# A two-layer hybrid decoder in float32: where the matmuls' moving operands stand in SBUF

## The reference, cut to what matters

```python
for layer in range(2):
    h = rmsnorm(x, g[0])
    m = mixer_ab(h, ...) if layer == 0 else mixer_cd(h, ...)
    x = x + rmsnorm(m, g[1])
    h = rmsnorm(x, g[2])
    x = x + rmsnorm(cross_attn(h, mem, wq, wkv, wo), g[3])   # 4 heads of 256
    h = rmsnorm(x, g[4])
    r = relu(h @ w1)                                         # 1024 -> 4096
    x = x + rmsnorm((r * r) @ w2, g[5])                      # 4096 -> 1024
```

## The kernel before

| moving operand, against | before | after |
|---|---|---|
| `h` (normed x; attention output), `w` | 448 | 448 |
| `r` (squared ReLU), `w` | 384 | 448 |
| `mem` (memory tokens), `w` (keys) | 256 | 448 |
| `mh`, `ml` (mixer C and D outputs), `w` | 256 | 448 |
| `my` (gated), `mp` (pooled), `w` | 320 | 448 |
| `k`, against `q` | 128 | 448 |
| `pt`, against `v` | 448 | 448 |
| `w`, against `mem` (values) | 256 | 64 |

## Time and profile before

### The profile page before, as it was taken

One profiled execution on the slowest core, in us unless ns is written; L12 is line 12 of the kernel. 1 busy time (PEld: TensorE's weight loads), 2 busy tenths in 40 slices (PEclk: granted clock), 3 DMA queues, 4 the chain that ended last, 5 costly groups with the idle time before them and its releaser, 6 DMA issues.

```text
span 960.5 us, 17149 instructions
## 1 busy us (share of the span) xinstructions
PE 902.9 (94%) x7268; PEld 878.1 (91%) x7268; DVE 667.1 (69%) x1030; ACT 472.7 (49%) x661; POOL 268.6 (28%) x195
## 2 busy tenths in 40 slices
PE   6999998899989999999999988999998699999997
PEld 6899988798979999999799988899898699999996
DVE  6897988777287555555779999967676385555553
ACT  5545544565355444444553333646464364454543
POOL 1000817243142000000468687346341340000000
PEclk9999999999999999999999999999999899999999
DMA  8454434544455555655555554245442445655551
GB/s 286 133 176 133 149 114 134 174 133 132 132 175 182 192 189 186 195 186 183 162 165 181 180 173 125 96 137 169 156 133 88 132 132 182 202 191 193 190 184 45
DMA packets 81031, 153.74 MB, mean 160 GB/s; under 512 B 6251, under 2 KB 7227, under 8 KB 80955
## 3 DMA queue, kind: packets, MB, share of 16 engines
q1 hardware_dynamic: 80843, 152.60, 49.9%
q10 hardware_dynamic: 112, 0.05, 0.0%
HBM read 151.58 MB, written 1.05 MB: 159 GB/s over the span
## 4 chain that ended last, share of the span: by engine, by line
PE 64%; DVE 24%; ACT 4%; issue 3%; POOL 3%; DMA 2%; DVEq 0%; POOLq 0%; ACTq 0%
PE ps L501 20%; PE ps L503 20%; PE ps L502 19%; DVE ps L1643 5%; DVE w_lo L1279 4%; ACT w_hi L927 2%; POOL w_lo L1916 2%; DVE E L1450 1%; DVE xc L1351 1%; DMA raw<-in_mlp_w 1%; DVE xT L1591 1%; PE ps L743 1%; PE ps L745 1%; PE ps L744 1%; PE ps L568 1%
## 5 line engine op out<-in xcount | busy, mean ns | idle before, releaser
L927 ACT ACTIVATE w_hi<-raw 128x1024 fp32r<-128x1024 f32 x284 | 296.9, 1055 | 255.8 <-DMA raw<-in_mlp_w 138.4
L501 PE MATMUL ps<-h_hi,w_hi 128*128 128x256 f32 x1280 | 363.8, 284 | 27.9 <-issue 13.7
L1279 DVE TENSOR_TENSOR w_lo<-raw,w_hi 128x1024 fp32r<-128x1024 f32 x210 | 274.1, 1324 | 129.5 <-ACT w_hi L927 129.3
L502 PE MATMUL ps<-h_lo,w_hi 128*128 128x256 f32 x1280 | 360.9, 282 | 0.0
L503 PE MATMUL ps<-h_hi,w_lo 128*128 128x256 f32 x1280 | 360.9, 282 | 0.0
L501 PEld LDWEIGHTS ps<-h_hi,w_hi 128*128 128x128 f32 x1280 | 247.1, 193 | 31.9 <-issue 17.8
L502 PEld LDWEIGHTS ps<-h_lo,w_hi 128*128 128x128 f32 x1280 | 247.3, 193 | 0.0
L503 PEld LDWEIGHTS ps<-h_hi,w_lo 128*128 128x128 f32 x1280 | 247.1, 193 | 0.0
L1916 POOL TENSOR_TENSOR w_lo<-raw,w_hi 128x1024 fp32r<-128x1024 f32 x74 | 183.0, 2494 | 99.4 <-ACT w_hi L927 99.4
L1939 POOL TENSOR_TENSOR rfac<-stat,mhalf 128x2 f32<-128x2 f32 (+1 forms) x14 | 16.6, 1182 | 457.1 <-DVE stat L1573 326.1
L501 PE MATMUL ps<-r_hi,w_hi 128*128 128x256 f32 x512 | 144.3, 282 | 0.0
(11 more groups left out here) (247 smaller groups left out, 1291.7 us busy)
## 6 DMA issues: line engine op xcount, KB each, us to landing
raw<-in_mlp_w SPq DMA_DIRECT2D x128, 512.0 KB, 3.8
raw<-in_cd_w_in SPq DMA_DIRECT2D x40, 512.0 KB, 3.7
raw<-in_xa_wkv SPq DMA_DIRECT2D x32, 512.0 KB, 4.0
raw<-in_ab_w_in SPq DMA_DIRECT2D x24, 512.0 KB, 3.9
raw<-in_xa_wq SPq DMA_DIRECT2D x16, 512.0 KB, 3.8
raw<-in_xa_wo SPq DMA_DIRECT2D x16, 512.0 KB, 3.8
raw<-in_cd_w_out SPq DMA_DIRECT2D x16, 512.0 KB, 3.7
raw<-in_ab_w_out SPq DMA_DIRECT2D x12, 512.0 KB, 3.8
```

The costliest lines, as they stand in the source:

```text
L501: nc.tensor.matmul(dst, wt[0], x[0], start=start, stop=False, skip_group_check=True)
L502: nc.tensor.matmul(dst, wt[0], x[1], start=False, stop=False, skip_group_check=True)
L927: nc.scalar.activation(w_hi[:, v % SLOTS, :, :], raw[:, v % SLOTS, :, :], ACT.Copy)\
L1279: V.tensor_tensor(w_lo[:, v % SLOTS, :, :], raw[:, v % SLOTS, :, :], f(w_hi[:, v % SLOTS, :, :]), ALU.subtract).then_inc(lo_ready_dve, 1)
```

## The change

It moves tensors and does nothing else: `mhalf` (8 floats) goes ahead of the memory tokens, and the unused bytes are placed anew, so that the places are those of the table's last column. No instruction is added, removed or moved in order.

```diff
--- before.py
+++ after.py
@@ -291,9 +291,9 @@
             raw = sb("raw", [SLOTS, 2, 512], scope=s)
         w_lo = sb("w_lo", [SLOTS, 2, 512], F32R)
         xT = sb("xT", [J, T])
-        skip(256)
+        mhalf = sb("mhalf", [8])
+        skip(416)
         mem_hi, mem_lo = sb("mem_hi", [J, T], F32R), sb("mem_lo", [J, T], F32R)
-        skip(192)
         h_hi, h_lo = sb("h_hi", [J, T], F32R), sb("h_lo", [J, T], F32R)
         k_hi, k_lo = sb("k_hi", [J, T], F32R), sb("k_lo", [J, T], F32R)
 
@@ -304,9 +304,7 @@
         Ssum, S2 = sb("Ssum", [H2]), sb("S2", [T])
         stat = sb("stat", [16, 8])
         rfac = sb("rfac", [16, 8])
-        mhalf = sb("mhalf", [8])
         tmp = sb("tmp", [2, T])
-        skip(352)
 
         with ExitStack() as s:
             v_hi, v_lo = sb("v_hi", [TT, D], F32R, s), sb("v_lo", [TT, D], F32R, s)
@@ -342,18 +340,19 @@
         with ExitStack() as s:
             vpad = sb("vpad", [J, T + 30], scope=s)
             cv, cv3 = sb("cv", [J, T], scope=s), sb("cv3", [J, T], scope=s)
+            skip(64, s)
             mh, ml = sb("mh", [2 * J, T], F32R, s), sb("ml", [2 * J, T], F32R, s)
             ppad = sb("ppad", [2, 2, T + 2], scope=s)
             sg = sb("sg", [4, T], scope=s)
             Rsq = sb("Rsq", [T], scope=s)
             sct = sb("sct", [2, H2], scope=s)
         with ExitStack() as s:
+            skip(64, s)
             q_hi, q_lo = sb("q_hi", [J, T], F32R, s), sb("q_lo", [J, T], F32R, s)
             prob = sb("prob", [4, TT, T], scope=s)
-            skip(448, s)
+            skip(384, s)
             pt_hi, pt_lo = sb("pt_hi", [4, TT, T], F32R, s), sb("pt_lo", [4, TT, T], F32R, s)
         with ExitStack() as s:
-            skip(64, s)
             r_hi, r_lo = sb("r_hi", [2, 4, T], F32R, s), sb("r_lo", [2, 4, T], F32R, s)
             relu, rsq = sb("relu", [2, H2], scope=s), sb("rsq", [2, H2], scope=s)
             otok = sb("otok", [TT, D], scope=s)
```

## The result

| | before | changed |
|---|---|---|
| median of 18 runs | 960.62 us | 964.87 us |
| lowest, highest | 957.85, 964.16 | 958.22, 969.37 |
| the profiled execution, own time and span | 962.23, 960.5 us | 962.71, 961.0 us |

The ratio is 1.0042, 95% interval 1.0029 to 1.0055. I had predicted 955.8 us, 948.5 to 961, with "slower" at 0.14. The changed kernel is slower. It came out as my second rival had it, both MLPs at the slow pace, for which I had 963.2 us and a chance of 0.12.

What follows compares the result with a forecast made beforehand. The prediction took PE's pace through pairs of load and matmul as the bound. Its terms, -4.1 + 1.7 - 1.3 - 0.3 = -4.0 us, took the 959.8 us median to 955.8, range 948.5 to 961.

Steps and rivals of the forecast that it cites:

- second rival: Both MLPs entered slow, so `h` behind the first MLP's sums loses 4.4 ns a matmul; 963.2 us, chance 0.12.
- PE's pace bounds the kernel, and it depends on place: PE busy 902.9 of 960.5 us; 113.4 or 117.8 ns a matmul at 320 and 448, 119 to 120 at multiples of 128.
- The first MLP is entered quick: Behind the first MLP's column sums all goes on at 113.4 ns; 768 matmuls of `r` save 4.1 us.
- the mixed case: The main forecast: first MLP at 113.4 ns, second at 117.8 ns behind its sums; 955.8 us, chance 0.48.
- The second MLP: Entered at 117.8 ns behind its column sums and kept there to the end, as no `r` at 384 resets it; +1.7 us.
- A pace lasts through `r` at 448: In both MLPs, a stream at 448 keeps the pace it starts with after a break; `r` there doesn't disturb it.
- the first rival: Both MLPs quick, the second by another start or a slow pace breaking off by itself; 949.4 us, chance 0.25.
- The other tiles save 1.6 us: Layer 1 from convolution to queries saves 1.3 us (`mh`, `mem` filler), scores 0.3 us, by leaving 119 to 120 ns.
- The values cost 0: Values, `w` moving against stationary `mem`, 256 to 64: no penalty seen at 256, 64 an odd multiple of 64; 0 us.
- Keys of layer 0 at 0: 192 matmuls of `mem` save PE up to 1.3 us, but its wait for DVE's sum grows by as much; 0 us.
- Runs further apart: Expected sign: times of single runs spread more than before, since nothing now resets the pace.
- The rule that speaks against it: Skill page's independent read ports for TensorE and PE never waiting: place changes nothing, sum 0 against 4.0 us by the rows.

Runs made afterwards that it cites:

- the kernel with `r` alone and a piece at 384: Kernel before with only `r` moved: `r` of `w2(0)` at 384, all later `r` at 448; 955.19 us, ratio 0.9943 to before.
- the kernel with late sums: Changed kernel with the MLP's column sums moved from between `w1(0)` and `w1(1)` to between `w2(6)` and `w2(7)`; 960.11 us, ratio 0.9953 to before.
- the one with two short stays at 384: Changed kernel with only the second half of `w2(0)`'s `r` at 384, two stays of 24 matmuls; 965.59 us, ratio 1.0040 to before.
- the kernel of before with late sums: Kernel before, `r` still at 384, with only the column sums moved to between `w2(6)` and `w2(7)`; 960.96 us, ratio 0.9996.

## Why the prediction was wrong, point by point

**PE's pace bounds the kernel, and it depends on place: right.** `r` alone, moved by 64 bytes, moves the time both ways, by what it leaves behind.

**The first MLP is entered quick: this step failed.** It is the term of -4.1 us. I wrote that the MLP is entered after column sums where PE had waited 0.16 us, and that all then goes on at 113.4. I read that wait as a fixed property and the quick piece behind it as its result. In the changed kernel PE came to the sums at 288.23 us without a wait, and the piece behind ran at 117.8 ns, as did all behind it. From the first matmul behind the sums to the end of `w2(7)`, with the clock at 1.00, it is 458.14 - 290.66 = 167.5 us before and 458.27 - 288.59 = 169.7 changed: +2.2 us, where I had -4.1 and the second rival +2.3. Over the 14 profiles that have the sums at the old place, the piece behind them was slow in 26 of 28 cases. The two quick ones are the first MLP of before and that of the kernel with `r` alone and a piece at 384, and the latter had no wait. In the kernel with late sums a break with a wait of 0.26 us came out slow. So a wait of that kind is neither needed for a quick start nor enough for one, and the quick entry of the first MLP was the exception. I had one profile with one quick and one slow entry, and should have given "both slow" at least the chance of the mixed case.

**The second MLP: right.** All came as forecast, 117.8 throughout and no piece of 11.4 us. From 781.15 to 938.58 us before, and from 780.12 to 939.29 changed, it is 157.4 and 159.2 us: +1.7, as in the sum.

**The size.** With +2.3 in place of -4.1 for the first MLP my own sum gives +2.3 + 1.7 - 1.6 = +2.4 us, and the rival has +3.4; the medians of 18 runs differ by 4.25. That near hit of the rival is in part luck. The 2.3 us holds against the one profile of before, whose first MLP was quick; where both are entered slow, as in most traces, the same terms give 1.7 + 1.7 - 1.6 = +1.8. What the rest of the 4.25 us is stays open.

**A pace lasts through `r` at 448: right in the MLPs, but not a law.** It lasted for both MLPs at 117.8 ns in the changed kernel and at 113.3 in the second MLP of the kernel with late sums. In the long stretch of `h` at 448 ahead of layer 1's convolution a slow stream can turn quick with no wait of PE, as the first rival had noted. Of the 16 profiles, 9 come slow and without a wait to the same border between two units there, after 528 matmuls of the stretch, and 7 of the 9 are quick a dozen matmuls on. The largest step between two starts at the border is 121 to 142 ns in the seven, and 119 and 126 in the two that stay slow. Windows on PE before, ahead of the border and behind it:

```profile
545.00:550.00 5.00, 5.00 (x45) 1.00 0.79 238
552.00:556.00 4.00, 4.00 (x38) 1.00 0.37 123
```

That is 5.28 / 45 = 117 and 4.28 / 38 = 113 ns. So a slip of PE by 3 to 24 ns went with another pace. Whether it is the slip that changes it was not tried, and one of 8 ns didn't.

**The other tiles save 1.6 us: the sum fits, not all of its parts.** With all moved but `r`, time x clock falls by 1.8 us (standard error 0.7), yet the time can't be told from before's. `mh` runs at 113 to 118 ns and no longer at 120, `mem` too. But `wo`, which I had at 0 within bounds, and the `h` behind the first scores, for which the sum has no term, lose 1.0 us. `mp`, at 320 before, was not to gain: one of its three stretches does (113 ns against 118), `my` doesn't.

**The values cost 0: wrong by 0.6 us.** They went from 227.9 to 231.1 ns over 192 matmuls. I had only a rough 216 to 225 ns from one window. My bound, "64 is an odd multiple of 64", was a rule made from too few places.

**Keys of layer 0 at 0: right.** PE's wait for the group sum grew from 1.0 to 1.8 us, and the gated piece begins as long after the keys as before.

**Runs further apart: open.** The standard deviation is 2.8 us against 1.6 for before over the 18 runs of each, and 3.5 against 2.2 when the changed kernel was run again. But it is 2.4 against 2.3 for `r` alone, which has the same slow MLPs, and 4.6 for the kernel with `r` back at 384, where most of it comes from the clock. With the clock's part taken out a wide spread remains for the changed kernel with late sums (4.5 us) and for the one with two short stays at 384 (3.7), against 2.0 for before.

**The rule that speaks against it.** The Trainium skill, page "SBUF — State Buffer", section "Who interferes with whom", says that PE never waits on anyone; taken at its word, the place would have no effect. The measurements decide against reading it so: the same loop takes 113.3 to 119.8 ns a matmul by the place of one tile alone. The page may well be right that no other engine is the cause; nothing here shows one.

**What stays open.** Why a break comes out quick or slow. What in the memory makes a place good or bad; only places were varied, not the layout of the weights. And whether the change makes the clock fall more often. The mean clock was below before's by 0.0003 to 0.0022 in the seven timed kernels with the other tiles moved, and by 0.0001 and 0.0002 with `r` alone, but also by 0.0012 in the kernel of before with late sums, which moves no tile. The standard errors are 0.0006 to 0.0012, so only the two values of 0.0022 stand out, at twice theirs. Near 140 us, where the wait for the group sum grew, 7 of the 12 profiles with the other tiles moved have a stretch at half clock, and 1 of the 4 others. That PE, done sooner, waits longer and the clock falls for it is one reading; it is not shown.

## What to carry to other kernels

When PE is busy all the time, measure the spacing from start to start for each pair of operands, not the duration, and compare pieces of the same loop. A placement that is good on the average may only keep whatever pace the stream happens to have: look at what sets the pace at a break, and at what used to reset it, before taking a "bad" place away. A deliberate bad piece right after the break (one of eight) made the good place pay: with `r` alone moved, 0.6% faster in place of 0.25% slower; in the changed kernel, 0.35% faster in place of 0.4% slower.

## What the runs showed of the hardware that was not expected

A stream of loads and 256-column fp32r matmuls can run at 113.3 or at 117.8 ns on the same addresses at full clock and hold either for over 160 us. Behind column sums it came out slow in 26 of 28 cases. A stay of 96 matmuls at 384 ended quick each time; two stays of 24 changed slow to quick and then quick to slow, in both MLPs of one kernel. At one place in the program a slow stream turned quick in 7 of 9 cases with no wait of PE, at a step of at most 142 ns. With `r` moved and the weights left, behind a quick piece, the pace repeats after 256 bytes in the four pairs of places tried, and steps of 32 bytes matter. With the weights moving, 512 columns took 227.9 ns with the memory tokens at 256, 231.1 at 64 and 233.2 at 192, so the good places of one kind of matmul are not those of the other.
